# A hybrid decoder step on one core: the gate weights all split, five low parts and half of the gate input's low part on GpSimd, one table set for the second q norm

## The reference, cut to what matters

```python
def hybrid_layer(x, cache_k, cache_v, h0_re, h0_im, p):
    z = rmsnorm(x, p['attn_norm_g']) @ p['w_in']
    q, k, v, u = split_projection(z)
    q = rmsnorm(q, p['q_norm_g'])
    k = rmsnorm(k, p['k_norm_g'])
    ...
    y_ssm, h_re, h_im = ssm_mixer(u, h0_re, h0_im, A_bar, B_bar,
                                  p['ssm_C_re'], p['ssm_C_im'], p['ssm_D'])
    g = jax.nn.gelu(y_ssm)
    ssm_out = (g * jax.nn.sigmoid(g @ p['w_glu'].astype(jnp.float32)
                                  + p['b_glu'].astype(jnp.float32))).astype(x.dtype)
    mix = jnp.concatenate([rmsnorm(attn, p['attn_out_g']),
                           rmsnorm(ssm_out, p['ssm_out_g'])], axis=-1)
    h = x + mix @ p['w_out']
    y = h + jnp.square(jax.nn.relu(rmsnorm(h, p['mlp_norm_g']) @ p['w_mlp_up'])) @ p['w_mlp_down']
    return y, new_k, new_v, h_re.astype(h0_re.dtype), h_im.astype(h0_im.dtype)
```

## Time and profile before

| | before |
|---|---|
| median of 3 runs | 1171.74 us (1171.49 to 1172.71) |
| profiled execution: time / span | 1173.1 us / 1171.3 us |
| PE busy, instructions | 1165.4 us (99%), 8510 |
| DVE busy | 748.5 us (64%) |
| ACT busy | 429.1 us (37%) |
| POOL busy | 138.5 us (12%) |
| mean granted TensorE clock | 0.999 |

### The profile page before, as it was taken

The page is one execution under the profiler, slowest core; times in us unless marked ns, Lnnn a source line. Parts: engine busy times, 40 slices in busy tenths (PEclk is TensorE's granted clock), DMA queues, the critical chain, the costliest instruction groups (busy, mean ns, idle before and its releaser), DMA issues.

```text
span 1171.3 us, 20412 instructions
## 1 busy us (share of the span) xinstructions
PE 1165.4 (99%) x8510; PEld 1102.1 (94%) x8510; DVE 748.5 (64%) x808; ACT 429.1 (37%) x520; POOL 138.5 (12%) x83
## 2 busy tenths in 40 slices
PE   9999999999999999999999999999999999999998
PEld 7676676899999999999999999999999999999998
DVE  7999999879775566544455545555654445555554
ACT  6110043875444333333334333333333332433331
POOL 0502602000000011000001000001100000100000
PEclk9999999999999999999999999999999999999999
DMA  7633334524554444645554455444455555445553
GB/s 293 188 128 108 130 124 143 184 76 156 189 171 168 162 162 144 197 163 165 170 170 145 162 188 171 163 162 162 144 183 177 164 170 168 145 163 184 171 167 118
DMA packets 55192, 190.30 MB, mean 162 GB/s; under 512 B 7864, under 2 KB 10168, under 8 KB 54712
## 3 DMA queue, kind: packets, MB, share of 16 engines
q1 hardware_dynamic: 54824, 188.80, 48.3%
q10 hardware_dynamic: 288, 0.30, 0.1%
HBM read 185.83 MB, written 5.28 MB: 163 GB/s over the span
## 4 chain that ended last, share of the span: by engine, by line
PE 97%; ACT 2%; DMA 1%; issue 0%; SPq 0%; DVE 0%; ACTq 0%
PE psum L1407 96%; ACT s_head L595 1%; DMA h_t<-in_x 1%; PE psum L1543 0%; ACT mov_b L565 0%; ACT s_samp L604 0%; ACT pt_head L614 0%; ACT L595 0%; ACT L571 0%; ACT L584 0%; ACT L538 0%; ACT au L538 0%; ACT au L584 0%; ACT u_t L571 0%; ACT w_hi L472 0%
## 5 line engine op out<-in xcount | busy, mean ns | idle before, releaser
L761 DVE TENSOR_TENSOR w_lo<-w_raw,w_hi 128x1024 fp32r<-128x1024 f32 x294 | 409.5, 1405 | 386.0 <-ACT w_hi L472 385.2
L1407 PE MATMUL psum<-mov_b,w_hi 128*128 128x288 f32 x2656 | 530.0, 296 | 0.2 <-ACT au L538 0.2
L472 ACT ACTIVATE w_hi<-w_raw 128x1024 fp32r<-128x1024 f32 x294 | 308.4, 1058 | 492.2 <-PE psum L1407 480.5
L1407 PEld LDWEIGHTS psum<-mov_b,w_hi 128*128 128x128 f32 x2656 | 425.7, 188 | 2.2 <-issue 1.0
L1407 PE MATMUL psum<-mov_a,w_hi 128*128 128x288 f32 x2048 | 406.6, 295 | 0.0
L1407 PE MATMUL psum<-mov_b,w_lo 128*128 128x288 f32 x1328 | 390.7, 294 | 0.0
L1407 PEld LDWEIGHTS psum<-mov_a,w_hi 128*128 128x128 f32 x2048 | 327.7, 188 | 0.1
L1407 PE MATMUL psum<-mov_a,w_lo 128*128 128x288 f32 x1024 | 300.7, 294 | 0.0
L1407 PEld LDWEIGHTS psum<-mov_b,w_lo 128*128 128x128 f32 x1328 | 251.2, 189 | 0.0
L1407 PEld LDWEIGHTS psum<-mov_a,w_lo 128*128 128x128 f32 x1024 | 193.3, 189 | 0.0
L1407 PE MATMUL psum<-x_g,w_raw 128*128 128x288 f32 x640 | 162.0, 410 | 0.5 <-ACT x_g L482 0.5
(11 more groups left out here) (180 smaller groups left out, 490.0 us busy)
## 6 DMA issues: line engine op xcount, KB each, us to landing
w_raw<-in_w SPq DMA_DIRECT2D x335, 512.0 KB, 3.3
h_t<-in_x SPq DMA_DIRECT2D x3, 576.0 KB, 9.2
out_y<-h_t SPq DMA_DIRECT2D x3, 576.0 KB
b_w<-in_b SPq DMA_DIRECT2D x1, 1024.0 KB, 7.6
c_w<-in_c SPq DMA_DIRECT2D x1, 1024.0 KB, 7.6
k_cache<-in_kc SPq DMA_DIRECT2D x1, 1024.0 KB, 5.6
v_cache<-in_vc SPq DMA_DIRECT2D x1, 1024.0 KB, 5.8
out_kc<-in_kc SPq DMA_DIRECT2D x1, 992.0 KB
```

Of the source, the lines that this page charges most:

```text
L472: nc.scalar.activation(hi3[:, n % SLOTS, :], raw3[:, n % SLOTS, :], ACT.Copy) \
L761: nc.vector.tensor_tensor(lo3[:, n % SLOTS, :], raw3[:, n % SLOTS, :], hi3[:, n % SLOTS, :].bitcast(F32), ALU.subtract) \
L1407: return nc.tensor.matmul(out, lhs_t, rhs, start=start, stop=stop)
```

## The change

- All four steps of glu0 are now split; no w_glu product is full.
- EARLY is now steps 40 to 43. ScalarE makes the high part of 42 before the squares of q, once VectorE has turned the last states out (the w_hi slots 2 and 3 lie over its tables), and that of 43 behind the squares.
- ScalarE loads the table set with both Ln and Exp by name, ahead of `hi_part(42)`.
- `u_his(1)` goes ahead of `exps(0, 1)`, and `pt_out(0)` ahead of `sample_exps`.
- GpSimd makes the low parts of steps 41, 42, 43, 44 and 45, and u_lo of half 1. VectorE keeps `lo_part(40)`, u_lo of half 0 and all from 46 on.
- PE does gate tile 4 ahead of the samples' scores, then 5 and 6, `turn_probs(0, 1)`, tile 7.

```diff
--- before.py
+++ after.py
@@ -88,7 +88,7 @@
 
 
 
-EARLY = (S_GLU, S_GLU + 1)
+EARLY = tuple(range(S_GLU, S_SPLIT))
 
 
 def hi_count(n):
@@ -571,12 +571,16 @@
                 nc.scalar.activation(part, part, ACT.Gelu_apprx_tanh).then_inc(gelu_ready, 1)
 
             gelu(0)
-            for n in EARLY:
-                hi_part(n)
+            hi_part(EARLY[0])
+            hi_part(EARLY[1])
+            nc.scalar.preload_act_table_set("natural_log_exp_and_others")
+            act.wait_ge(turned_out, 8)
+            hi_part(EARLY[2])
 
             unit_read(act, UNIT["g_q1"])
             for at in (0, 2):
                 nc.scalar.activation(au3[:, at:at + 2, :], q3[:, 4 + at:6 + at, :], ACT.Square).then_inc(squared, 1)
+            hi_part(EARLY[3])
             unit_full(act, UNIT["y1"])
             u_his(0)
             head_scale(UNIT["qn1"], au3, 4)
@@ -658,13 +662,13 @@
                     nc.scalar.activation(b4[:, first + k, 0, :], src[:, k, :], ACT.Copy,
                                          scale=gain_column(name, k)).then_inc(mix_hi, 1)
 
+            u_his(1)
             exps(0, 1)
-            u_his(1)
             hi_part(S_SPLIT)
             exps(1, 2)
             hi_part(S_SPLIT + 1)
+            pt_out(0)
             sample_exps(3)
-            pt_out(0)
             gate_out(0)
             hi_part(S_SPLIT + 2)
             hi_part(S_SPLIT + 3)
@@ -1142,15 +1146,9 @@
                     .then_inc(probs_ready, 1)
 
             dve.wait_ge(last_copied, 8)
-            def u_los(half):
-                dve.wait_ge(u_hi, half + 1)
-                part = b4[:, 4 * half:4 * half + 4, :, :]
-                tt(part[:, :, 1, :], u3[:, 4 * half:4 * half + 4, :], part[:, :, 0, :].bitcast(F32), ALU.subtract) \
-                    .then_inc(u_lo, 1)
-
             lo_part(EARLY[0])
-            u_los(0)
-            lo_part(EARLY[1])
+            dve.wait_ge(u_hi, 1)
+            tt(b4[:, 0:4, 1, :], u3[:, 0:4, :], b4[:, 0:4, 0, :].bitcast(F32), ALU.subtract).then_inc(u_lo, 1)
             soft_max(0)
             q_norm(1, au3)
             dve.wait_ge(q_blk_zero, 1)
@@ -1167,8 +1165,6 @@
             sample_max()
             soft_scale(1, 2)
             sample_scale(3)
-            lo_part(S_SPLIT)
-            lo_part(S_SPLIT + 1)
 
             def prompt_out(g):
 
@@ -1233,7 +1229,6 @@
 
             gate_mul(0)
             soft_max(2)
-            u_los(1)
             lo_part(S_SPLIT + 2)
             mix_los(gate3, "g_ssm", 0, range(2))
             lo_part(S_SPLIT + 3)
@@ -1372,12 +1367,26 @@
                        ot6[:, k % 2, :, NCHUNK - 1, :, DEC_SEQ - 1:CHUNK:DEC_SEQ], ALU.add) \
                         .then_inc(last_copied, 1)
 
+            def lo_part(n):
+
+                pool.wait_ge(hi_split, hi_count(n))
+                tt(lo3[:, n % SLOTS, :], raw3[:, n % SLOTS, :], hi3[:, n % SLOTS, :].bitcast(F32), ALU.subtract) \
+                    .then_inc(lo_split[n % SLOTS], 1)
+
             for half in range(2):
                 add_turned(half)
                 copy_last(half)
+            lo_part(EARLY[1])
             pool.wait_ge(last_copied, 8)
             unit_full(pool, UNIT["y1"])
             nc.gpsimd.memset(q_blk[:, :], 0.0).then_inc(q_blk_zero, 1)
+            lo_part(EARLY[2])
+            lo_part(EARLY[3])
+            pool.wait_ge(u_hi, 2)
+            pool.wait_ge(u_lo, 1)
+            tt(b4[:, 4:8, 1, :], u3[:, 4:8, :], b4[:, 4:8, 0, :].bitcast(F32), ALU.subtract).then_inc(u_lo, 1)
+            lo_part(S_SPLIT)
+            lo_part(S_SPLIT + 1)
 
             def add_group(g, unit, buf, past=0):
 
@@ -1560,12 +1569,7 @@
                 done.then_inc(psum_full, 1)
 
             def glu(m, tiles):
-                if m == 0 and tiles.stop <= STEP_K * len(EARLY):
-                    gemm(UNIT["glu0"], S_GLU, HALF_STEPS, b4, ready=tiles_ready(u_lo, per=4), part=tiles)
-                elif m == 0:
-                    gemm_full("glu0", S_GLU, HALF_STEPS, u3, tiles_ready(gelu_ready, per=4), tiles)
-                else:
-                    gemm(UNIT["glu1"], S_SPLIT, HALF_STEPS, b4, ready=tiles_ready(u_lo, per=4), part=tiles)
+                gemm(UNIT[f"glu{m}"], S_GLU + HALF_STEPS * m, HALF_STEPS, b4, ready=tiles_ready(u_lo, per=4), part=tiles)
 
 
             pe.wait_ge(warm_filled, 1)
@@ -1637,6 +1641,7 @@
             glu(0, range(0, 2))
             scores(1)
             glu(0, range(2, 4))
+            glu(0, range(4, 5))
             u = UNIT["ssc"]
             unit_free(pe, u)
             pe.wait_ge(qblk_ready, 1)
@@ -1647,9 +1652,9 @@
                     mm(out[:, 0:WINDOW], qb4[:, g, n, :], kc4[:, g, n, :])
                     done = mm(out[:, WINDOW:WINDOW + SAMPLE], qb4[:, g, n, :], kv3[:, g, SEQ:TOK])
             done.then_inc(psum_full, 1)
-            glu(0, range(4, 6))
+            glu(0, range(5, 7))
             turn_probs(0, 1)
-            glu(0, range(6, 8))
+            glu(0, range(7, 8))
             pe.wait_ge(q_ready, 2)
             scores(2)
             glu(1, range(0, 3))
```

## The result

The changed kernel takes **1173.47 us** (median of 22 runs, 1173.12 to 1175.10) against 1171.82 us before (22 runs on the same chip, 1171.26 to 1173.42). The ratio is **1.0015, 95% interval 1.0009 to 1.0021**: 1.65 us longer, within the 0.2% that I set as the bound. The profiled execution has a time of 1173.57 us and a span of 1171.7 us.

A forecast was written before the change was run, and what follows sets the result against it. PE bounds the kernel, busy 1165.4 of 1171.3 us, but ScalarE sets glu1's start. GpSimd's holds on VectorE delay the gate by 1.4, samples' scores by 3.7, transposes by 2.95, glu1 by 1.9: 1173.6 us, range 1170.8 to 1175.6.

The forecast's parts named there:

- u_los(0) ends: VectorE's low part before the gate, held by GpSimd's low part of step 42: ends at 202.4 instead of 200.2.
- first gate tile on PE: PE's gate start, waiting for VectorE's u_los(0): 202.45 against 201.04, +1.4 us.
- u_lo of half 1 in time: GpSimd's low part for the fifth gate tile: PE would not wait for it, in time by over 1 us.
- samples' scores: PE's scores behind soft_max(1)'s bank: 213.55 instead of 209.88, +3.7 us, with PE waiting 1.2.
- transposes done, next tile: PE's turned probabilities after two split tiles: done at 219.45 instead of 216.50, +2.95 us.
- gate_out(0) done, glu1 starts: ScalarE's pt_out, sample_exps and gate_out, 4.8 us, then PE's second gate half: 224.25 against 222.31, +1.9 us.
- on the median: The whole kernel: the +1.9 us at glu1 put on the median 1171.74, giving 1173.6 us.
- The second hold: GpSimd's u_lo of half 1 goes between VectorE's q norm instructions and holds the rest for 2.6 us.
- the preload falls into a wait for a weight load: ScalarE's table load at about 188.5 us would stand in such a wait and cost nothing.
- one hold dodged: Case in which only the second hold counts, u_los(0) being ready 0.2 us earlier: +0.5 us; chance 0.08.
- The known fall goes away: Rival: PE's clock fall at 251.30 is missed as the samples' outputs shift: -1.7, so +0.2, 1171.9; chance 0.12.
- The clock falls in a new place: Rival: new waits, one before the samples' scores, bring one more PE clock fall: +3.6 us, 1175.3; chance 0.22.

The follow-up runs named there:

- e2: Kernel before plus one GpSimd subtraction of 1024 columns into an unused buffer, behind the memset of q_blk; 1173.49 us, ratio to before 1.0016.
- e8: Changed kernel with GpSimd's low parts timed into VectorE's PSUM reads, step 43's back on VectorE, gate_out(0) ahead of sample_exps, other reorderings; 1170.17 us, ratio to before 0.9987.
- e1: Changed kernel, with GpSimd starting the low part of step 42 only when VectorE has done u_los(0); 1174.14 us, ratio to before 1.0022.
- e4: Changed kernel without the named table load, so logarithm and exponential have a load each again; 1174.82 us, ratio to before 1.0029.
- e7: Changed kernel, with GpSimd starting u_lo of half 1 only after the q norm and the copies into q_blk; 1173.25 us, ratio to before 1.0014.
- e6: Kernel before with the named table load alone added; 1171.79 us, ratio to before 0.9998.
- e3: Kernel before plus two GpSimd subtractions into an unused buffer, the second timed to the end of soft_max(0); 1176.38 us, ratio to before 1.0036.

## Why the prediction was right

Forecast 1173.6 us in 1170.8 to 1175.6, most of the chance on a change within 0.2%; measured 1173.47. By its own steps:

| step | predicted | measured |
|---|---|---|
| u_los(0) ends | 202.4 | 202.46 |
| first gate tile on PE | 202.45 | 202.60 |
| u_lo of half 1 in time | PE does not wait | no wait |
| samples' scores | 213.55, behind a wait of 1.2 | 213.38, 0.91 |
| transposes done, next tile | 219.45 | 219.24 |
| gate_out(0) done, glu1 starts | 224.25 | 224.26, 224.31 |
| on the median | +1.9 | +1.65 |

**What carried it** was the reading of the earlier trace rows: that a GpSimd instruction on SBUF tensors and a VectorE instruction with two of them exclude each other for a whole instruction. e2 shows that one such GpSimd instruction costs 1.7 us with nothing else changed, e8 that moving them, with the other edits named there (by the rows gate_out's place is worth some 1.5 us of it), turns the loss into a gain. The Trainium skill (SBUF — State Buffer, section "SBUF: two separate sides") adds that the instruction of VectorE with two SBUF inputs is held only by a GpSimd operation that reads SBUF. Here the memset at 197.52, which reads nothing, left VectorE's low part beside it at 1.22 us, and the two low parts behind it did not leave u_los(0) alone: the trace agrees.

**Steps that were off.** The second hold was put at a full 2.6 us and is 2.38 (4.18 less 1.80), which with 0.05 the other way elsewhere gives 213.38 for 213.55. Four places of VectorE's row, not two, were touched: I had not priced the 8-column TENSOR_SCALAR (+0.5 us at 213.36) nor soft_scale(1) beside the low part of step 45 (+2.2 us at 218.62). Both were harmless here, since PE needs neither at once. In e1 the same kind of hold decided, in e4 it did so together with ScalarE's two loads, and there my expectation failed; in e7 it stood where I had expected it and cost PE nothing. The prediction also said that the preload falls into a wait for a weight load. The wait there was for VectorE (7.25 us, the first row), and in the changed kernel the load, at 188.49, is followed by one of 4.82 us for VectorE; it cost nothing all the same.

**The "one hold dodged" case** (+0.5) is not what dodging gives: e1 takes the first hold away and lands at +2.1 (224.37), e7 the second and lands at +1.55 (223.86).

**The clock.** "The known fall goes away" was priced at 1.7 us and given 0.12. The last column of the table prices it at 1.5 to 1.6: 947.3 to 947.5 us behind glu1's start in eight kernels, 949.0 and 948.9 in before and e6, the two profiles with the fall at about 251 us. It did not decide the medians: three runs of the 22 after and four of the 22 before lie more than 0.5 us above the rest of theirs, so it seems to come in few executions of either. The recorded mean granted clock of after's three is 0.999, that of its other nineteen 1.000. The profiled execution of before, at 1173.1 us, is such an execution, 1.4 us above the median of 1171.74 beside it, and the comparison of the two profiles alone would have said +0.4 us for a change that costs 1.65. This also shows a slip in the pricing: the -1.7 was taken off a forecast for the median, while the median of before lies among the executions without the fall, so that its going away could save the median nothing. "The clock falls in a new place" did not happen in the profiled execution of after; where the three slower ones lost their clock is not recorded. e3 shows that it exists, at 1.4 us, behind a wait of 2.47 us rather than 0.91.

**Open.** Why the fall comes in one execution of a kernel and not in the next, and where in the kernel the upper half of e1's executions lost their clock.

## What to carry to other kernels

Before work is given to an idle GpSimd, list what VectorE runs at that time, and place it beside instructions that read PSUM: unplaced, six instructions of 2.4 to 2.8 us cost this kernel 1.65 us, placed by waits (with one of the five low parts back on VectorE and three small reorderings, ScalarE's gate_out above all) the same idea gained 1.5. Look for such a hold in the durations of both engines, not in the waits, and follow a moved one to the next meeting before you count it as gone. And where one profile is set against another, check first that both have the same granted clock in the stretch behind the change.

## What the runs showed of the hardware that I had not expected

- An 8-column float32 TENSOR_SCALAR on one SBUF tensor is held like the large ones: 0.17 us free, 0.68 after and 1.53 in e1. In both it ends 0.03 us behind GpSimd's instruction (214.04 against 214.01, 205.40 against 205.37): its cost is what is left of that instruction, whatever its own size.
- Where both engines had such work queued they took turns, one instruction each: after, u_los(0) ends at 202.46 and GpSimd's second low part 2.25 us behind it (198.00 + 6.71 = 204.71), one whole low part, so it began only then.
- After a wait of 2.47 us PE's granted clock averaged 0.57 in the next 3 us and 0.86 in the 3 us behind (e3); at 2.58 us (e1) and at 1.65 us (after) the profiled execution kept 1.00. The length of the wait alone does not tell.
